# A transformer stack on one core: the block input's region moved to a multiple of 128 bytes, and the conditioning at the start divided and loaded in another order

## What is computed

```
c_act = silu(c)
mod = c_act @ w_ada + b_ada                    # 1024 x 6144
sh_m, sc_m, gt_m, sh_f, sc_f, gt_f = split(mod, 6)
h = rms_norm(x, g_pre_mix) * (1.0 + sc_m) + sh_m
y = mixing_sublayer(h, ...)                    # h @ w_in, pooling, dilated attention, @ w_out
x = x + gt_m * rms_norm(y, g_post_mix)
h = rms_norm(x, g_pre_ffn) * (1.0 + sc_f) + sh_f
x = x + gt_f * rms_norm(conv_ffn(h, ...), g_post_ffn)
# second block: h = rmsnorm(x, g); ten projections of h, three branches, w_out, and a second conv_ffn
```

## Time and profile before

| | us |
|---|---|
| median of 3 runs | 1664.28 (1662.15 to 1668.35) |
| the profiled execution | 1666.63 |
| its span, first to last instruction | 1664.8 |
| PE busy in the span | 1555.7 (93%) |
| POOL busy | 713.9 |
| ACT busy | 664.9 |
| DVE busy | 588.2 |

### The profile page before, as it was taken

How to read it: one execution, slowest core, us unless ns; L and a number is a source line. 1 busy time by engine, 2 the same in 40 slices (tenths; PEclk the granted TensorE clock), 3 DMA queues, 4 the chain that set the end, 5 groups by cost and what they waited for, 6 DMA issues and landing times.

```text
span 1664.8 us, 19895 instructions
## 1 busy us (share of the span) xinstructions
PE 1555.7 (93%) x7670; PEld 1260.4 (76%) x7670; DVE 588.2 (35%) x928; ACT 664.9 (40%) x987; POOL 713.9 (43%) x608
## 2 busy tenths in 40 slices
PE   7899978899999999999989889999899999999996
PEld 4699757688888888788855568787687788887885
DVE  3665442523333100422034430342325555555001
ACT  2442453444444322322344443453333555544231
POOL 0467103535545544545411136335524554455442
PEclk8999987999999999999999999999999999999999
DMA  8463015322232223234210123122311222322221
GB/s 368 159 271 141 27 68 110 82 98 82 94 101 88 85 86 95 76 102 135 84 45 30 38 102 115 51 76 80 132 55 51 86 90 101 101 81 83 90 86 65
DMA packets 28491, 162.73 MB, mean 98 GB/s; under 512 B 4584, under 2 KB 4840, under 8 KB 13704
## 3 DMA queue, kind: packets, MB, share of 16 engines
q1 hardware_dynamic: 24960, 151.05, 26.4%
q10 hardware_dynamic: 3464, 10.74, 2.5%
HBM read 157.04 MB, written 4.74 MB: 97 GB/s over the span
## 4 chain that ended last, share of the span: by engine, by line
PE 70%; issue 10%; POOL 8%; DVE 6%; DMA 3%; ACT 2%; POOLq 0%; SPq 0%; ACTq 0%; DVEq 0%
PE ps L1693 60%; POOL WL L774 7%; DMA adaw<-w_ada_dram 2%; PE ps L1659 1%; PE ps L1902 1%; DMA raw<-w_up_dram 1%; PE ps L1916 1%; PE ps L1929 1%; DVE S L1584 1%; POOL WL L738 1%; DVE ps L1299 1%; DVE S L1571 1%; PE ps L1826 1%; DVE xT L1304 1%; DVE md L1574 0%
## 5 line engine op out<-in xcount | busy, mean ns | idle before, releaser
L738 POOL TENSOR_TENSOR WL<-raw,WH 128x512 fp32r<-128x512 f32 (+2 forms) x344 | 369.7, 1103 | 584.2 <-ACT WH L854 584.1
L1693 PE MATMUL ps<-hH,WH 128*128 128x512 f32 x1136 | 461.1, 406 | 22.2 <-POOL hL L752 9.3
L1693 PE MATMUL ps<-hL,WH 128*128 128x512 f32 x1136 | 453.9, 400 | 0.0
L1693 PE MATMUL ps<-hH,WL 128*128 128x512 f32 x1136 | 453.4, 399 | 0.0
L774 POOL TENSOR_TENSOR WL<-raw,WH 128x512 fp32r<-128x512 f32 x176 | 246.3, 1430 | 253.9 <-ACT WH L1014 253.9
L1693 PEld LDWEIGHTS ps<-hH,WH 128*128 128x128 f32 x1136 | 216.8, 191 | 79.5 <-issue 25.3
L1693 PEld LDWEIGHTS ps<-hH,WL 128*128 128x128 f32 x1136 | 216.6, 191 | 53.2
L1693 PEld LDWEIGHTS ps<-hL,WH 128*128 128x128 f32 x1136 | 216.8, 191 | 50.4
L854 ACT ACTIVATE WH<-raw 128x1024 fp32r<-128x1024 f32 (+3 forms) x172 | 148.1, 885 | 234.8 <-PE ps L1693 231.2
L1693 PE MATMUL ps<-hidH,WH 128*128 128x512 f32 x352 | 137.9, 392 | 1.1 <-POOL WL L774 1.1
L1693 PE MATMUL ps<-hidL,WH 128*128 128x512 f32 x352 | 137.0, 389 | 0.0
(11 more groups left out here) (275 smaller groups left out, 2221.9 us busy)
## 6 DMA issues: line engine op xcount, KB each, us to landing
raw<-w_up_dram SPq DMA_DIRECT2D x44, 1024.0 KB, 4.9
raw<-w_in_dram SPq DMA_DIRECT2D x36, 1024.0 KB, 4.9
adaw<-w_ada_dram SPq DMA_DIRECT2D x20, 1024.0 KB, 7.1
raw<-w_down_dram SPq DMA_DIRECT2D x16, 768.0 KB, 4.2
raw<-w_down_dram SPq DMA_DIRECT2D x16, 640.0 KB, 3.9
adap<-w_ada_dram SPq DMA_DIRECT2D x4, 1024.0 KB, 18.1
xT<-x_dram ACTq DMA_DIRECT2D x2, 2048.0 KB, 10.2
raw<-w_mem_kv_dram SPq DMA_DIRECT2D x4, 1024.0 KB, 4.7
```

Of the source, the lines that this page charges most:

```text
L738: pool.tensor_tensor(WL[:, d % 2, ks, cols], raw[:, d % 2, ks, cols], WH[:, d % 2, ks, cols].bitcast(F32), ALU.subtract).then_inc(lo_done, 1)
L1693: mm = pe.matmul(out, lhs[x], rhs[y], start=(first and i == 0), stop=(last and i == 2))
```

## The change

Three things are changed. The region `front` begins at a multiple of 128 bytes: `xT` at 20224 = 158 x 128 in place of 20160; everything behind the region stays where it was. Block 0 moves from PE to VectorE, so VectorE makes three blocks before the projections in place of two (2 and 0 ahead of `norm`, 3 behind the first half of `apply`) and PE one in place of two (block 1, whose two halves are separate steps now). And SP's loads stand in another order. The warming matmuls are 45 and 8 in place of 30.

```diff
-ADA_DVE = (2, 3, 4, 5, 6, 7, 8, 9, 10, 11)
-ADA_PE = (0, 1)
-ADA_FIRST, ADA_REST = 2, 8
+ADA_DVE = (2, 0, 3, 4, 5, 6, 7, 8, 9, 10, 11)
+ADA_PE = (1,)
+ADA_FIRST, ADA_REST = 3, 8
...
-        front = (nc.sbuf_base + 31) // 32 * 32
+        front = (nc.sbuf_base + 127) // 128 * 128
...
-        steps = [("start",), ("warm", 30), ("ada_row", 0), ("ada", 0), ("ada", 1)]
-        steps += [("squares", N_PRE1, k) for k in range(KD)] + [("ada_turn", 0), ("row_turn", 0), ("ada_turn", 1)]
-        steps += [("norm", N_PRE1), ("split", 0), ("ada_end", 0), ("apply", N_PRE1, 0, 4), ("ada_row", 1), ("seg", D_IN, 0, 0, 4)]
-        steps += [("row_turn", 1), ("ada_end", 1), ("apply", N_PRE1, 4, KD), ("split", 1)]
+        steps = [("start",), ("warm", 45), ("ada", 0), ("ada", 1)]
+        steps += [("squares", N_PRE1, k) for k in range(KD)] + [("ada_turn", 0), ("ada_turn", 1), ("ada_row", 0, 0), ("norm", N_PRE1), ("split", 0)]
+        steps += [("ada_end", 0), ("apply", N_PRE1, 0, 4), ("ada", 2), ("warm", 8), ("seg", D_IN, 0, 0, 4), ("ada_row", 0, 1), ("row_turn", 0)]
+        steps += [("ada_turn", 2), ("ada_end", 1), ("apply", N_PRE1, 4, KD), ("split", 1)]
...
-            ada_row(0)
-            ada(0)
-            ada(1)
-            ada(2)
-            load(0)
-            ada_row(1)
-            ada(3)
+            for piece in range(4):
+                ada(piece)
+            load(0)
+            ada_row(0)
+            ada(4)
+            ada(5)
             load(1)
...
-                    ve.wait_ge(ada_turned, part + 1)
-                    ve.wait_ge(row_turned, part + 1)
+                    ve.wait_ge(ada_turned, part + 2)
+                    if part == 1:
+                        ve.wait_ge(row_turned, 1)
```

More of the change, by code:

```diff
@@ L163, in build @@
         small = sb("small", [P, 64])
-        front = (nc.sbuf_base + 31) // 32 * 32
+        front = (nc.sbuf_base + 127) // 128 * 128
         tile_bytes = 4 * KD * S
         ctx.enter_context(nc.sbuf_tensor("front", [P, 3 * KD * S + 16], F32))
+        assert front + 3 * tile_bytes <= nc.sbuf_base and nc.sbuf_base % 128 == 0
         xT = nc.alloc_sbuf_tensor_at("xT", [P, KD, S], F32, offset=front)
@@ L1609, in _, with ada_row @@
         def _(pe):
[L1610 to L1615, removed]
+            def ada_row(n, part):
+                pe.wait_ge(adap_loaded[2 * n + part], 16)
+                for k in range(part * ADA_K, (part + 1) * ADA_K):
                     mm = pe.matmul(ps[0:1, 2 + 5 * n, :], small[:, 32 + k:33 + k], adap[:, n, k, :], start=(k == 0), stop=(k == KD - 1))
-                mm.then_inc(row_summed, 1)
+                if part == 1:
+                    mm.then_inc(row_summed, 1)
             def row_turn(n):
```

## The result

| | before | after |
|---|---|---|
| median us | 1665.19 (1662.15 to 1668.35, 4 runs) | 1639.20 (1637.40 to 1642.97, 4 runs) |
| span of the profiled execution, us | 1664.8 | 1637.9 |

The ratio of after to before is 0.984, with a 95% interval of 0.9818 to 0.9863: 26.0 us faster by the medians, 26.9 by the spans. The forecast was 27.9.

The account below looks back on a forecast made before the run. PE, busy in 200.00 of 200 us of the up projection, was taken as the bound. Part A -20.5, Part B +2.4 and Part C -9.8 give -27.9 us, 1636.4 on the median's scale; 8-in-10 range 1629 to 1649.

Parts of the forecast that it names:

- The bound: Dense stages: PE busy in 200.00 of 200 us at full clock, so each product's cost is the kernel's; POOL next.
- Part A: Dense products moving `front` rows: address at a multiple of 128 saves 6.6 ns each, 20.5 us in all (19.1 to 22.5).
- theory M: Follow-up's theory: for 512 columns only the moving operand's own offset counts; with `front` and weights 64 past, about 1657 us.
- a gap from the number of columns alone: Dense matmuls: equal columns give equal gaps, so the address does nothing; 1654.5, up to 1657 us; chance 0.11.
- Part B: Products by token, `hH` or `hpH` standing: the new address costs 2.3 ns each, 2.4 us at most over 1056.
- slower rival: Products on `front`: operands at the same offset collide, 4.6 ns each, 15.7 us more; 1672.6 us; chance 0.02.
- Costing the other engines at nothing: Dense stages: other engines' reads and writes of `front` lie beside PE and were priced at zero.
- Part C: The opening: new block division and load order start the second half at 46.9 against 56.68, 9.8 us gained (6 to 12).
- new wait in front of the norm: Opening, PE's queue: half a row product waits for its load at 24.8, takes 3.6, and costs 1.9 us of the gain.
- the step from the spread to `dl`: Opening: first `dl` starts 1.5 us after the norm's spread, as in the kernel before, so at 31.0.
- The sum: Whole kernel: -20.5 + 2.4 - 9.8 = -27.9 us, giving 1636.4 on the median's scale.
- The lead lasts: Behind the opening: order is unchanged and loads land earlier too, so the opening's 9.8 us shift should last.

Follow-up runs that it names:

- align_only: The kernel before with only `front` moved to a multiple of 128 bytes; 1647.73 us, ratio to before 0.9894.
- w64_h64: The changed kernel with `front` back at 64 past a multiple of 128 and `raw`, `WH`, `WL` also 64 past; 1642.4 us, one run.
- after_again: The changed kernel measured once more, unchanged, on the chip of some later runs; 1638.06 us, ratio to before 0.9823.
- open_only: The changed kernel with `front` back at its old address, so only the new opening remains; 1657.51 us, ratio to before 0.9956.
- row_after_norm: The changed kernel with both halves of PE's row product behind the norm's spread and without the 8 warming matmuls; 1636.04 us, ratio to before 0.9821.

## Why the prediction was right, and where not

- **The bound.** Right: PE's gap in the dense stages set the time. POOL took none of the gain (98.78 us of 200, as before).
- **Part A, the size.** 6.6 ns a product and 20.5 us were forecast. The leads give 21.0 net behind the units by token; those of `align_only`, 20.3.
- **Part A, the cause.** Half wrong. The step was "only the moving tensor differs, and it lies at a multiple of 128". The rows had two properties in one: `hid` and `mg` lay at a multiple of 128, and at the same offset as the weights. The runs with moved weights show that the place relative to the weights counts: by theory M `w64_h64` would have come near 1657 us and came at 1642.4. The change gave `front` both properties at once, so the forecast came out in spite of the wrong half; that is luck. The Trainium skill's rule of a gap from the number of columns alone (page "TensorE: Matmul & The Clock Gate", "Back-to-back issue gap"), stated for isolated matmuls and weighed as a rival, doesn't carry over to these pairs of loads and matmuls: equal columns took 226.7 or 233.3 ns.
- **Part B.** Right in sign and size: 2.2 ns against 2.3 forecast, which makes 2.3 us over 1056 products. Equal offsets are what it has in common with A, with the other sign, and the prediction's slower rival ("equal offsets collide") was right about 256 columns and wrong about 512.
- **Costing the other engines at nothing.** One term was missing: PE's wait for GpSimd's copies, 1.9 us in the group's row against 0.8 in all before, 0.7 net in the lead. It doesn't come from the address, but from which pattern two engines fall into. The fall of the clock in unit 8, 1.4 us, is the other term that the sum doesn't have.
- **Part C.** 9.8 forecast, 8.3 in after's profile, 10.0 in `after_again`'s and 9.8 in `open_only`'s. The new wait in front of the norm was there. Its load landed 0.7 later than worked out (25.5 for 24.8), and the product took 5.29 in place of 3.6 in after's profile, since the clock fell while it ran; the prediction had that in the range and not in the value. These 2.4 us became 1.4 at the first `dl` (32.40 for 31.0), because a third term was wrong the other way: 1.5 us were taken from the kernel before for the step from the spread to `dl`, and it took 0.5. The difference is VectorE's operation for `colA`, of before and of after:

```profile
41.91 1.21 DVE L1236 SCALAR_TENSOR_TENSOR colA<-mod,vec 128x4 f32<-128x4 f32 x1
```

```profile
32.20 0.16 DVE L1237 SCALAR_TENSOR_TENSOR colA<-mod,vec 128x4 f32<-128x4 f32 x1
```

  Why it varies is open; in `row_after_norm` it took 1.26.
- **The sum.** 26.9 by the spans against 27.9 is closer than its terms. The opening fell 1.5 short, and copies and clock took 2.1 that nobody had priced. Against that stand 1.3 in unit 1, where the kernel before lost clock, about 0.9 more from part A and 0.4 less lost to part B.
- **The lead lasts.** Right; in `open_only` it was 9.8 at the second half and 8.9 to 11.5 at every later stage.

## What to carry to other kernels

Where PE is busy all the time, compare the distance between starts of the same matmul on different tensors: a few nanoseconds on thousands of instructions were two thirds of this gain, and the busy share showed none of it. For 512 float32 columns let the moving tensor and the weights begin at the same place; here they were whole KiB apart, and distances of 32, 64 and 96 bytes cost 2 to 7 ns. For 256 columns measure both. And look at what stands in a queue ahead of a step whose operand is ready: a product whose load comes last belongs behind it.

## What the runs showed of the hardware that I had not expected

- The gap between matmuls depends on where its two operands begin relative to each other. With 512 columns moving: 226.7 ns when whole KiB apart; 233.3 to 234.3 for `h` at 32, 64 or 96 bytes off; 229.0 and 233.3 for `hid` with the weights at 64 and 96. With 256 columns: 119.9 when whole KiB apart, 116.9 to 119.9 for `h`, 113.4 and 118.3 for `bufA`.
- Copies of 128x512 on VectorE took 0.56 us alone, and 0.6 or 1.1 beside GpSimd's, in two patterns that came with either address of `front`.
- PE's clock fell to 0.50 in one profile and not in another of the same kernel, after the same waits of 0.6 to 0.7 us: 5.29 and 3.59 us for the same eight matmuls.
